# Attention scores split over row halves and strips, and small products of the token stage spread over strips and halves

## The reference, cut to what matters

```
kk = l2_normalize(heads(k * k_k))                       # 6 heads of 64
w = exp(-DECAY_SCALE * sigmoid(decay_w0[d] + tanh(lw) @ decay_up[d]))   # 64 -> 384, d = 0, 1
a = sigmoid(iclr_a0[d] + la @ iclr_up[d])                               # 64 -> 384, d = 0, 1

s = einsum('bqhd,bkhd->bhqk', q, k) * scale             # 6 heads, d = 96 = 64 (nope) + 32 (rotary)
p = softmax(s);  o = einsum('bhqk,bkhd->bqhd', p, v)    # v: 64 columns a head
```

## Time and profile before

| | |
|---|---|
| median of three runs | 5467.54 us |
| the profiled execution | 5469.95 us |
| its span | 5467.9 us |
| PE busy | 5195.8 us, 95% |
| DVE, ACT, POOL busy | 52%, 38%, 12% |
| mean granted TensorE clock | 0.977 |

### The profile page before, as it was taken

One profiled execution on the slowest core, in us unless ns is written; L12 is line 12 of the kernel. 1 busy time (PEld: TensorE's weight loads), 2 busy tenths in 40 slices (PEclk: granted clock), 3 DMA queues, 4 the chain that ended last, 5 costly groups with the idle time before them and its releaser, 6 DMA issues. The chain is left out here.

```text
span 5467.9 us, 94771 instructions
## 1 busy us (share of the span) xinstructions
PE 5195.8 (95%) x38844; PEld 2846.5 (52%) x38844; DVE 2824.3 (52%) x4438; ACT 2067.2 (38%) x3470; POOL 641.8 (12%) x1110
## 2 busy tenths in 40 slices
PE   8999999989989999989989999999899799999899
PEld 3444444478865555544444444444778655555454
DVE  2221486645545555556522214776455455555565
ACT  1211555345544444421112114553455444444211
POOL 0000000044430000001100000000445300000011
PEclk9999999999999999999999998999999999999999
DMA  5311565465541111036343115654656411110353
GB/s 225 140 67 56 182 214 193 142 169 148 159 122 48 25 42 31 6 116 221 118 160 140 70 55 181 214 193 144 169 144 165 120 45 25 43 31 6 107 174 117
DMA packets 570089, 646.07 MB, mean 118 GB/s; under 512 B 228336, under 2 KB 455152, under 8 KB 559872
## 3 DMA queue, kind: packets, MB, share of 16 engines
q1 hardware_dynamic: 569072, 638.88, 37.3%
q10 hardware_dynamic: 592, 1.15, 0.1%
HBM read 372.77 MB, written 267.13 MB: 117 GB/s over the span
## 5 line engine op out<-in xcount | busy, mean ns | idle before, releaser
L490 PE MATMUL ps<-feat_hT,w_features 128*128 128x512 f32 x2240 | 972.5, 592 | 0.0
L808 PE MATMUL ps<-w_tokens,prep_hT 128*128 128x512 f32 (+1 forms) x1920 | 826.9, 590 | 23.3 <-DMA prep_hT<-s_ht 23.3
L1701 PE MATMUL ps<-att_K,att_Q 96*128 96x512 f32 x1632 | 744.9, 599 | 31.9 <-DMA att_K<-s_qkt 22.2
L490 PEld LDWEIGHTS ps<-feat_hT,w_features 128*128 128x128 f32 x2240 | 420.4, 190 | 505.9 <-issue 502.8
L1813 DVE TENSOR_REDUCE att_mx<-ps 128x1 f32<-128x1024 f32 x384 | 470.3, 1225 | 291.0 <-PE ps L1701 291.0
L808 PEld LDWEIGHTS ps<-w_tokens,prep_hT 128*128 128x128 f32 x1920 | 365.8, 192 | 476.1 <-issue 450.1
L2094 PE MATMUL ps<-w_out,fin_yT 128*128 128x512 f32 x1280 | 569.5, 598 | 2.5 <-DVE fin_yT L2044 2.5
L1708 PEld LDWEIGHTS ps<-kc,att_pr 128*128 128x128 f32 x3264 | 367.4, 141 | 277.4 <-issue 231.5
L1777 ACT ACTIVATE att_PT<-ps 128x512 f32<-128x512 f32 x384 | 228.9, 596 | 642.1 <-PE ps L1708 641.3
L1701 PEld LDWEIGHTS ps<-att_K,att_Q 96*128 96x128 f32 x1632 | 297.3, 192 | 334.7 <-issue 276.2
L1768 ACT ACTIVATE att_pr<-ps,att_nb 128x1024 f32<-128x1024 f32 x384 | 424.4, 1110 | 80.2 <-DVE att_nb L1815 80.1
(11 more groups left out here) (226 smaller groups left out, 6794.8 us busy)
## 6 DMA issues: line engine op xcount, KB each, us to landing
s_sc<-prep_sc SPq DMA_DIRECT2D x20, 3072.0 KB, 9.2
scan_src<-s_sc SPq DMA_DIRECT2D x160, 384.0 KB, 4.9
s_qkt<-scan_qT SPq DMA_DIRECT2D x40, 576.0 KB, 4.1
fin_z<-s_zt SPq DMA_DIRECT2D x40, 576.0 KB, 5.2
s_zf<-feat_co SPq DMA_DIRECT2D x88, 256.0 KB, 2.5
s_ht<-feat_hT SPq DMA_DIRECT2D x10, 2048.0 KB, 7.9
prep_hT<-s_ht SPq DMA_DIRECT2D x40, 512.0 KB, 5.7
s_zt<-prep_st SPq DMA_DIRECT2D x80, 256.0 KB, 3.4
```

Source lines behind the costliest of these rows:

```text
L490: last = pe.matmul(b, wf[:, k, i * P:(i + 1) * P], hT[g % 2][:, k, :], start=(k == 0), stop=(k == KD - 1))
L808: last = pe.matmul(ps[:, tiles.bank(pieces[n]), 0:c1 - c0], hT[j % NH][:, k, :], wt[:, k, c0:c1], start=(k == 0), stop=(k == KD - 1))
L1701: pe.matmul(ps[:, c, :], Q[:, t * P:(t + 1) * P], K[:, k0:k0 + G], start=True, stop=True).then_inc(scored, 1)
```

## The change

Scores: outside the very first slot of a layer, each product of 96 rows becomes one of 64 rows (nope) and one of 32 rows (rotary) that accumulate in the same bank. Queries are kept twice (both row halves) and four times (all four strips of 32 rows); each half holds the keys of two groups, each strip those of one. The order in a slot is: two products in the two halves (banks 0, 1), four in the four strips (banks 0 to 3), two in the two halves (banks 2, 3). Every copy is a transfer of its own: 18 for a head in place of two. The buffers of even heads lie in the memory of w_out, which is loaded later, when head 4 has been scored. Since the strips hold the key groups in the order 0, 2, 1, 3, the rows of V are picked in that order.

Token stage: norm now fills 70 columns (six heads at offsets 0, 32, 64), so that the inverse norms lie in three strips, and inv takes one strip for each m; a of direction 0 and w of direction 1 alternate over m, and so do their sigmoids on ScalarE and their places in the order of banks.

```diff
             uses.add(("a", g, 0, m), "act")
-        for m in range(BA):
             uses.add(("w", g, 1, m), "act")
...
-        norm = sb("norm", [HA, G])
+        norm = sb("norm", [NR, G])
...
-                    sigmoids("a", g, 0)
-                    sigmoids("w", g, 1)
+                    for m in range(BA):
+                        sigmoid("a", g, 0, m)
+                        sigmoid("w", g, 1, m)
...
-                        last = pe.matmul(b[0:HA, :], kc[:, K_HS + m * HA:K_HS + (m + 1) * HA], tmp[:, m, :], start=(m == 0), stop=(m == BA - 1))
+                        last = pe.matmul(b[0:NR, :], kc[:, K_HS + m * NR:K_HS + (m + 1) * NR], tmp[:, m, :], start=(m == 0), stop=(m == BA - 1))
...
-                        pe.matmul(bank_free(u), kc[0:HA, K_HT + m * P:K_HT + (m + 1) * P], norm[:, :], start=True, stop=True).then_inc(filled, 1)
-                    lora("a", g, 0)
-                    lora("w", g, 1)
+                        b = bank_free(u)
+                        pe.matmul(b, kc[32 * m:32 * m + HA, K_HT:K_HT + P], norm[32 * m:32 * m + HA, :], start=True, stop=True).then_inc(filled, 1)
+                    for m in range(BA):
+                        lora("a", g, 0, m)
+                        lora("w", g, 1, m)
...
+    HALF = (slice(0, DN), slice(DN, P))
+    STRIP = [slice(DR * n, DR * (n + 1)) for n in range(4)]
+    KEYS = (0, 2, 1, 3)
...
+                def load_queries(h, c0, c1, sem):
+                    w, rows = heads_in[h % 2], d["qkt"][h * DQK:(h + 1) * DQK, c0:c1]
+                    for r in HALF:
+                        sp.dma_start(w[r, Q_N + c0:Q_N + c1], rows[0:DN, :]).then_inc(sem, 16)
+                    for r in STRIP:
+                        sp.dma_start(w[r, Q_R + c0:Q_R + c1], rows[DN:DQK, :]).then_inc(sem, 16)
...
+                def load_keys(h, sem):
+                    w, rows = heads_in[h % 2], d["qkt"][(HB + h) * DQK:(HB + h + 1) * DQK, T0:T]
+                    for n, r in enumerate(HALF):
+                        sp.dma_start(w[r, K_N + T0:K_R], rows[0:DN, 2 * G * n:2 * G * (n + 1)]).then_inc(sem, 16)
+                    for n, r in enumerate(STRIP):
+                        sp.dma_start(w[r, K_R + T0:K_R + T0 + G], rows[DN:DQK, G * n:G * (n + 1)]).then_inc(sem, 16)
...
-                load_qk(0, 0, T0, first_in)
-                load_qk(0, T0, T, arrived[0])
+                for n in range(2):
+                    sp.dma_start(first[:, n, :], d["qkt"][HB * DQK * n:HB * DQK * n + DQK, 0:T0]).then_inc(first_in, 16)
+                load_queries(0, T0, T, arrived[0])
+                load_keys(0, arrived[0])
...
-                        pe.matmul(ps[:, c, :], Q[:, t * P:(t + 1) * P], K[:, k0:k0 + G], start=True, stop=True).then_inc(scored, 1)
+                    def rows64(c):
+                        t, k0 = (c, 0) if s == 0 else (TPG - 1 + s, T0 + G * (KEYS[c] % 2))
+                        q, k = w[HALF[c % 2], Q_N + t * P:Q_N + (t + 1) * P], w[HALF[c % 2], K_N + k0:K_N + k0 + G]
+                        return pe.matmul(ps[:, c, :], q, k, start=(c < 2), stop=(c >= 2))
+                    def rows32(c):
+                        t, k0 = (c, 0) if s == 0 else (TPG - 1 + s, T0)
+                        r = STRIP[KEYS[c]]
+                        return pe.matmul(ps[:, c, :], w[r, Q_R + t * P:Q_R + (t + 1) * P], w[r, K_R + k0:K_R + k0 + G], start=(c >= 2), stop=(c < 2))
+                    for c in range(2):
+                        freed(c)
+                        rows64(c)
+                    for c in range(4):
+                        if c >= 2:
+                            freed(c)
+                        last = rows32(c)
+                        if c < 2:
+                            last.then_inc(scored, 1)
+                    for c in range(2, 4):
+                        rows64(c).then_inc(scored, 1)
```

More of the change, by code:

```diff
@@ L501, in token_projection @@
     PER = 10
+    NR = 32 * (BA - 1) + HA
     pieces = [(n, c, min(c + 512, WT)) for n in range(NT) for c in range(0, WT, 512)]
@@ L704, in empty, with sigmoid @@
                     a.activation(st[:, n % NB, 0:c1 - c0], ps[:, tiles.bank(pieces[n]), 0:c1 - c0], ACT.Copy).then_inc(z_out, 1)
-                def sigmoids(kind, g, e):
+                def sigmoid(kind, g, e, m):
                     out, c = {"w": (sg, C_W0), "a": (aa, C_A0)}[kind]
[L708 to L711, removed]
+                    u = (kind, g, e, m)
+                    a.wait_ge(filled, uses.ready(u))
+                    a.activation(out[:, m, :], ps[:, uses.bank(u), :], ACT.Sigmoid, bias=col[:, c + e * BA + m:c + e * BA + m + 1]).then_inc(act_out, 1)
                 def powers(g, e):
@@ L778, in _ @@
                     a.wait_ge(scaled_out, 2 * g + 1)
-                    sigmoids("a", g, 1)
+                    for m in range(BA):
+                        sigmoid("a", g, 1, m)
                     empty(n + 4)
@@ L815, in bank_free, with lora @@
                     return ps[:, uses.bank(u), :]
-                def lora(kind, g, e):
+                def lora(kind, g, e, m):
                     n = "wa".index(kind)
-                    for m in range(BA):
-                        b = bank_free((kind, g, e, m))
-                        pe.matmul(b, dup[DH * e:DH * e + DH, n, m * P:(m + 1) * P], low[DH * e:DH * e + DH, n, :], start=True, stop=True).then_inc(filled, 1)
+                    b = bank_free((kind, g, e, m))
+                    pe.matmul(b, dup[DH * e:DH * e + DH, n, m * P:(m + 1) * P], low[DH * e:DH * e + DH, n, :], start=True, stop=True).then_inc(filled, 1)
                 def blocks(g, e):
@@ L854, in _ @@
                         pe.wait_ge(up, 32)
-                    lora("w", g, 0)
+                    for m in range(BA):
+                        lora("w", g, 0, m)
                     pe.wait_ge(rk, g + 1)
@@ L1624, in sb @@
             return ctx.enter_context(nc.sbuf_tensor(f"att{l}_" + name, shape, F32))
-        Qs = [sb(f"Q{b}", [DQK, T]) for b in range(2)]
-        Ks = [sb(f"K{b}", [DQK, T]) for b in range(2)]
+        heads_in = (late[0][:, :, :].rearrange("p k n -> p (k n)"), sb("qk", [P, 2 * T + 2 * T0 + 3 * G])[:, :])
+        first = sb("first", [DQK, 2, T0])
+        Q_N, Q_R, K_N, K_R = 0, T, 2 * T, 2 * T + T0 + 2 * G
         Vs = [sb(f"V{b}", [P, NT, DV + 1]) for b in range(2)]
@@ L1679, in _ @@
                         sp.wait_ge(summed, GROUPS * (h + 1))
-                        load_qk(h + 2, 0, T, arrived[h % 2])
+                        load_head(h + 2, arrived[h % 2])
                         load_v(h + 2)
+                    if h == LAST_IN_WO:
+                        sp.wait_ge(scored, 4 * NSLOT * (h + 1))
+                        sp.dma_start(wo[:, :, :], d["w_out"][:, l * KD:(l + 1) * KD, :]).then_inc(late_in, 16)
                     sp.wait_ge(normed, GROUPS * (h + 1))
```

47 lines of the change are left out of this document (29 added, 18 removed).

## The result

The changed kernel takes 5423.43 us, the median of four runs (5420.43 to 5432.90); the kernel before takes 5465.65 us, the median of the four beside it. The ratio is 0.9928 with an interval of 0.9913 to 0.9943. The forecast was 5422.

| stage, by PE's starts, us | layer 1 before, after | layer 2 before, after | both, change | forecast |
|---|---|---|---|---|
| feature_projection | 535.6, 538.8 | 520.2, 517.9 | +0.9 | 0 |
| token_projection | 547.2, 526.4 | 546.6, 526.0 | -41.4 | -37.5 |
| rwkv_scan (not touched) | 527.2, 525.9 | 529.0, 543.2 | +12.9 | 0 |
| mla_attention | 782.1, 778.0 | 783.1, 777.3 | -9.9 | -7.5 |
| out_projection | 355.0, 356.0 | 324.4, 324.1 | +0.7 | 0 |

The account below looks back on a forecast made before the run. PE, busy 95% of the span, bounds the kernel. Slots -14, prompt slots +3.5, transfers +3 and token stage -37.5 give -45 against 5469.95: 5425, or 5422 for the median (chance 0.62); range 5385 to 5490.

Parts of the forecast that it names:

- The change of tile size: On PE, each change of tile size costs a 0.10 us drain plus an uncovered first load of 0.05 to 0.11.
- The slot: Attention scores: 3.37 us in place of 3.44, 0.07 saved a slot, 14 us over 202 slots.
- Prompt slots: Attention: products wait 0.2 and 0.15 us for banks still being read, in ten such slots, +3.5 us.
- The heads of the stages: Attention start: head 0's larger transfer delays the second slot, +3 us for two layers, bounds 0 and +14.
- The token stage: inv to next projection: 5.97 us, 3.6 saved in each of ten groups; -37.5 us with the other terms, bounds -44 and -17.
- the one behind the stretches: Projections behind four token-stage stretches lose 6 us at the low clock; 2 of them counted as saved.
- a shorter six-row stretch: Token stage: the clock mostly stays up because inv's six-row stretch shrinks from 2.8 to 1.1 us.
- Rival 1: Attention scores: halves and strips change without a drain, saving 81 us more, 5341; chance 0.07.
- Rival 2: Attention strips: loads overlap only in part, 0.14 us a slot, +28 us, 5450; chance 0.08.
- Rival 3: Attention strips don't run four at a time: 5487 with serial loads, 5595 two at a time; chance 0.09.
- Rival 4: Token stage: the clock falls as before, -17 in place of -37.5 us, 5442; chance 0.09.
- Rival 5: Attention: the clock falls because PE stands still 0.8 us a slot, +139 us, 5561; chance 0.05.

Follow-up runs that it names:

- experiment 6: The changed kernel with the half products of all four banks first and the strip products last in each slot; 5440.72 us, ratio 0.9953 to the kernel before.
- experiment 2: The kernel before with only the attention part of the change, token stage as before; 5456.39 us, ratio 0.9981.
- experiment 9: The changed kernel plus 44 one-column products at the head of layer 1's output projection, where PE waits anyway; 5408.18 us, ratio 0.9895 to the kernel before.
- experiment 3: The kernel before with norm and inv in three strips, but a and w in the old order, attention as before; 5432.71 us, ratio 0.9941.
- Experiments 3 and 5: experiment 3, and the kernel before with inv's three products still one after another but over 128 rows, extra rows meeting zero weights; the latter 5446.35 us, ratio 0.9964.
- the other kernels with a shift of 80: Other kernels whose added instructions put layer 2's program about 80 past its old place in the 256-instruction pieces; scan of layer 2 from 532.8 us.
- experiment 4: The kernel before with only the alternation of a and w over m, inv as before; 5454.86 us, ratio 0.9983.

## Why the prediction was right

**The change of tile size** was read right: the drain and first load were put at 0.19 to 0.21 a group, and the starts show halves, strips, halves at 1.06, 1.07, 1.06 where 1.07, 1.07, 1.07 were forecast. Start to start less the streamed columns, the four kinds of change take 0.09 to 0.10 us each (64 to 32 rows 0.092, back 0.091, 64 to 128 rows 0.093, 128 to 64 rows 0.096, medians of 200 or more). By the Trainium skill (TensorEngine Tiling (Array Packing), Key Properties) a change of the tiling mode drains TensorE; the trace agrees for 64 to 32 rows, which no row of before showed, and experiment 6 gives the price of a whole group in tiles of its own a second way: 0.20 for the drain and the first load together, as forecast.

**The slot** gained 0.10, not 0.07: the terms for the bare loads behind the last group and for the staggered starts (0.06 and 0.03 in the sum) were a little high. Over both layers the slots behind the first two gain 17.1 us; the forecast had 14 - 3.5 = 10.5.

**Prompt slots** were right. A bank is wanted before its exponential has been read, and the groups there take 1.28 and 1.34 in place of 1.06 and 1.07:

```profile
1990.65 1.35 PE L1746 MATMUL ps<-att_qk 64*128 64x512 f32 x4
1991.93 1.41 PE L1751 MATMUL ps<-att_qk 32*128 32x512 f32 x8
1993.27 1.13 PE L1746 MATMUL ps<-att_qk 64*128 64x512 f32 x4
```

Of the two periods around it one is 0.39 longer than before and one 0.21 shorter, 0.38 more than two other slots, which are 0.10 shorter each. 0.35 was forecast, in ten places.

**The heads of the stages** were under-sized for the profiled execution: the first two periods of the two layers are 4.2 and 3.0 us longer, 7.2 where 3 were forecast, inside the bound of 14. The transfer did become the releaser, as forecast, but it landed at 14.6 us after the first slot and not at 12: the window has 215 GB/s, the sum had 243 from the earlier trace rows. The term varies with the execution: the second slot came 13.2 and 14.1 us after the first in experiment 2, and 13.0 and 12.0 in experiment 9, with the same transfers; the same two periods are 3.6 us longer in all in experiment 2 and 1.0 in experiment 9, so the 3 lies among what was measured.

**The token stage** is the largest term, and right in its mechanism. The stretch was forecast at 5.97 and takes 5.93 in all ten. The mis-sized term is the one behind the stretches: of the 6 us that projections lose at the low clock I counted 2 as saved, and all of it was. 36.5 us of stretches and 6 behind them make 42.5; norm's wider loads take some 0.3 back (2.70 in place of 2.67, ten times), and 41.4 were measured. Experiments 3 and 5 part the sum, taken in this order, by the token stages of both layers:

| step | token stages, both | gain |
|---|---|---|
| before | 1093.8 | |
| 128 rows in inv: the clock stays up | 1070.1 | 23.7 |
| inv in three strips at once | 1053.9 | 16.2 |
| a and w alternate | 1052.4 | 1.5 |

So more than half comes from the clock, if it is counted first. The prediction gave that the right sign with a reason (a shorter six-row stretch) that the runs neither need nor refute: with full rows the stretch is as long as before and the clock stays up too. It gave the order of a and w little, and that was right.

**What was missing** is the scan, 12.9 us over both layers, all of it in layer 2. Against the forecast of -45 for the profiled execution the terms are: token stage 3.9 us better, slots 6.6 better, heads 4.2 worse, the scan 12.9 worse, the untouched stages together 1.3 worse; 8 us worse in all. The median, 9.5 below that execution, hides it: the forecast of the median is right within 2 us by a sum with errors in it both ways, and that closeness is luck. Where the median execution is shorter isn't known; in the scan of layer 2 the other kernels with a shift of 80 are 4 to 13 us longer than before. No row of before could give the missing term a size.

**The rivals.** Rival 1 (no drain, 5341) falls by the starts, 0.09 a change. Rival 2 (loads bare, or strips at 3.07 times, 5450) falls by the 1.07 of the strips: with their load and drain they take no longer than two halves, streaming alone 0.86 for eight records of 0.43, which is four times. The Trainium skill (TensorE: Matmul & The Clock Gate, Measured speedup vs the span model) has 3.07. An estimate from that page's figure gives the group 1.12 + 0.21 us, and the measured 1.07 decides. Counted with drain and load, 3.44 / 1.07 = 3.2. Rival 3 (not four at a time, 5487 or more) falls by the same row. Rival 4 (the clock falls in the token stage, 5442) falls by PEclk 1.00 in ten windows; experiment 4 shows what it looks like. Rival 5 (it falls in attention) falls by the window over all slots behind the head:

```profile
1640.00:2386.00 746.00, 724.60 (x4110) 0.99 0.18 42
```

## What to carry to other kernels

Price a split into tiles by groups, not by products: here a group in tiles of its own cost 0.86 us of streaming and 0.2 of change whether it held two products or four, so three groups in place of four products of 0.86 were worth 0.10 us of 7.2. Small products that use few rows are dear beyond their own time if the clock falls behind them; giving them all rows costs nothing in time and made the token stages 23.7 us shorter here, and the order came to only 1.5 us after that. A saving on one engine's stream is worth its price only where no bank is still being read: in experiment 6 0.20 us saved a slot became a loss. When a stage that nobody touched changes, look at where TensorE's program is cut into pieces: a few idle instructions in a place where TensorE waits moved the median by 15 us, and a comparison of two kernels of this length within 0.3% should be made at more than one such place.

## What the runs showed of the hardware

- Six matmul records of six rows, 2.7 to 3.3 us, were followed by a fall of the granted clock from 2.4 to 1.2 GHz in nineteen of twenty stretches (before and experiment 4). The same six records with 128 rows were followed by none in ten; with the three products side by side in strips (1.06 us), none in the twenty of experiment 3 and of the changed kernel.
- Idle times of 1.6 to 3.6 us at the ends of 256-instruction pieces, in a stage with some 43 instructions a us on PE. The Trainium skill (Runtime: NRT & Kernel Launch, Instruction fetch mechanics) has the pieces, and says that crossing an end costs "one DMA tail-bump, mostly hidden". The trace agrees on the size of the pieces (326 packets of 16 KB for PE's 83520 records) and not on the cost: 16 to 31 us for 90 ends in a stage, where the 90 steps just ahead of these take 2 us. In or right behind the longest of them the granted clock fell as well, 20 times in the fourteen scans of layer 2.
- Strips of 32 rows that write four different banks over 128 columns each start within some 20 ns of each other and stream at the rate of one (the next four start 0.53 us after the first, 0.43 of streaming and 0.10 of the group's first load).
